# A decoder trunk on one core: compression's first unit, its cache copies, the third sequence's pages and gelu's table

## The reference

```python
h = x @ w_in                                  # q, k, v of all heads, gate logits
o_A = dilated window attention (8 heads)
# compression: 32 rows of 64, every 16 rows, of the paged cache and of the new rows
blk = rows[:, idx] + pe[:, None, :]
kc  = gelu(blk @ w1) @ w2                     # likewise vc
o_B = gated sum of compressed, selected (top 16 blocks) and window attention
x = LayerNorm(alpha*x + concat(o_A, o_B) @ w_o)
x = LayerNorm(alpha*x + PEER(x))              # top 16 of 128*128 experts per head
```

## Time and profile before

| what | us |
|---|---|
| median of 3 runs (1332.22 to 1334.04) | 1333.13 |
| the profiled execution's own time | 1332.8 |
| its span in the trace | 1331.0 |
| TensorE busy in the span | 1271.3 (96%) |
| VectorE | 974.2 (73%) |
| ScalarE | 573.7 (43%) |
| GpSimd | 294.5 (22%) |
| mean granted TensorE clock | 0.987 of full |

### The profile page before, as it was taken

One profiled execution on the slowest core, in us unless ns is written; L12 is line 12 of the kernel. 1 busy time (PEld: TensorE's weight loads), 2 busy tenths in 40 slices (PEclk: granted clock), 3 DMA queues, 4 the chain that ended last, 5 costly groups with the idle time before them and its releaser, 6 DMA issues.

```text
span 1331.0 us, 25923 instructions
## 1 busy us (share of the span) xinstructions
PE 1271.3 (96%) x8435; PEld 1081.4 (81%) x8436; DVE 974.2 (73%) x2220; ACT 573.7 (43%) x1058; POOL 294.5 (22%) x521
## 2 busy tenths in 40 slices
PE   9998599989899999999999999999999999999996
PEld 6888588866554777889998889889889888988985
DVE  4664366546634399989988887887888788888886
ACT  4643366534421211124345454454455444444453
POOL 0004132040001288711121111111122112212101
PEclk9998799999999999999999999999999999999998
DMA  8756577788974487859939999989988999998962
GB/s 289 225 160 190 167 248 243 261 276 325 403 303 167 144 285 287 290 199 260 287 122 330 318 311 315 319 312 312 321 309 308 323 312 309 322 317 301 324 196 92
DMA packets 164384, 358.79 MB, mean 270 GB/s; under 512 B 49235, under 2 KB 99091, under 8 KB 160595
## 3 DMA queue, kind: packets, MB, share of 16 engines
q1 hardware_dynamic: 134562, 242.51, 53.8%
q0 software_dynamic: 25424, 111.37, 23.9%
q10 hardware_dynamic: 4320, 3.93, 0.9%
HBM read 341.56 MB, written 53.35 MB: 297 GB/s over the span
## 4 chain that ended last, share of the span: by engine, by line
PE 50%; DVE 4%; issue 2%; DVEq 1%; ACT 1%; POOLq 0%; POOL 0%; ACTq 0%
PE psum L1918 25%; PE psum L1907 7%; PE psum L1906 7%; PE psum L1905 7%; PE psum L1427 2%; PE psum L1931 2%; DVE gated_i L2066 2%; DVE v_lo L2079 0%; DVEq L2066 0%; ACT v_hi L1987 0%; DVE OT L2062 0%; DVE ln_bn L1354 0%; DVE x L1348 0%; DVE gated_lo L2115 0%; DVE x L1377 0%
## 5 line engine op out<-in xcount | busy, mean ns | idle before, releaser
L1907 PE MATMUL psum<-x_hi,u_lo 128*128 128x256 f32 x760 | 215.1, 283 | 0.0
L1906 PE MATMUL psum<-x_lo,u_hi 128*128 128x256 f32 x760 | 215.0, 283 | 0.0
L1905 PE MATMUL psum<-x_hi,u_hi 128*128 128x256 f32 x760 | 214.6, 282 | 0.0
L2079 DVE TENSOR_TENSOR v_lo<-big,v_hi 128x1024 fp32r<-128x1024 f32 x128 | 156.7, 1224 | 35.1 <-ACT v_hi L1987 33.8
L1987 ACT ACTIVATE v_hi<-big 128x1024 fp32r<-128x1024 f32 x128 | 135.3, 1057 | 83.1 <-PE psum L1918 80.9
L1918 PE MATMUL psum<-v_hi,gated_hi 128*128 128x512 f32 x512 | 159.9, 393 | 1.1 <-DVE gated_lo L2115 1.0
L1918 PE MATMUL psum<-v_lo,gated_hi 128*128 128x512 f32 x512 | 158.7, 390 | 0.0
L1918 PE MATMUL psum<-v_hi,gated_lo 128*128 128x512 f32 x512 | 158.3, 390 | 0.0
L1906 PEld LDWEIGHTS psum<-x_lo,u_hi 128*128 128x128 f32 x760 | 145.5, 191 | 3.7
L1905 PEld LDWEIGHTS psum<-x_hi,u_hi 128*128 128x128 f32 x760 | 145.5, 191 | 3.7
L1907 PEld LDWEIGHTS psum<-x_hi,u_lo 128*128 128x128 f32 x760 | 145.5, 191 | 0.0
(11 more groups left out here) (323 smaller groups left out, 2518.8 us busy)
## 6 DMA issues: line engine op xcount, KB each, us to landing
big<-in_peer_v SPq DMA_DIRECT2D x128, 512.0 KB
big<-in_peer_u SPq DMA_DIRECT2D x115, 512.0 KB, 5.1
w_then_a_vals<-in_a_v SPq DMA_DIRECT2D x8, 2048.0 KB
keep_ak<-in_a_k POOLq DMA_DIRECT2D x32, 508.0 KB, 6.3
keep_av<-in_a_v POOLq DMA_DIRECT2D x24, 512.0 KB, 7.4
big<-in_a_k SPq DMA_DIRECT2D x4, 2048.0 KB, 13.3
a_keys<-in_a_k SPq DMA_DIRECT2D x4, 2048.0 KB, 12.4
wq_ring<-in_peer_wq SPq DMA_DIRECT2D x16, 512.0 KB, 5.6
```

What stands on the lines that cost most here:

```text
L1905: pe.matmul(H[:, 0:SEQ], uh[:, q, kc], x1h[:, k, :], start=(k == 0), stop=False)
L1906: pe.matmul(H[:, 0:SEQ], uh[:, q, kc], x1l[:, k, :], start=False, stop=False)
L1907: mm = pe.matmul(H[:, 0:SEQ], ul[:, q, kc], x1h[:, k, :], start=False, stop=(k == KD - 1))
L2079: ve.tensor_tensor(vl[:, q], vs[:, q], vh[:, q].bitcast(F32), ALU.subtract).then_inc(s["v_lo"], 1)
```

## The change

Four edits, all in the functions above:

- VectorE makes U0's quarters 1, 2 and 3 one after the other at the start of compression. Its gates come behind the bias copies.
- GpSimd's copies: none in U0 and U5; 32 (numbers 48 to 79) in U1 to U4, two per step, and ahead of steps 1 to 3 a wait for TensorE's step before. Numbers 32 to 47 go to the first norm, four ahead of each right part and four behind the last.
- The selected pages of sequence 2 are issued by ScalarE, two in each of four steps from U6's step 2 to U7's step 1, behind a wait for the prompt's last scores.
- ScalarE runs gelu on one column of a small tile of its own ahead of the real gelu in step 3, so that the table is loaded without the waits for TensorE and for the bias. The tile is filled once with a copy.

```diff
-def load_sel_pages(eng, t, d, s, b):
-
-    for p in range(PAGES):
+def load_sel_pages(eng, t, d, s, b, places=range(PAGES)):
+
+    for p in places:
         r = eng.value_load(t.ptab[0:1, b * PAGES + p:b * PAGES + p + 1], min_val=0, max_val=79)
...
+        warm = sb("gelu_warm", [P, 2])
...
             sp.dma_start(t.ka[1], d.a_k[1]).then_inc(s["ld_ka1"], 16)
-            load_sel_pages(sp, t, d, s, 2)
             sp.wait_ge(s["pages_lo"], 4 * NUC)
             load_sel_pages(sp, t, d, s, 1)
...
                 for j in range(4):
-                    for x in range(2 if u < 6 else 0):
-                        keep_copy(gp, d, s, 32 + 8 * u + 2 * j + x)
+                    if 1 <= u < 5:
+                        if j:
+                            rows_used(gp, u, j - 1)
+                        for x in range(2):
+                            keep_copy(gp, d, s, 48 + 8 * (u - 1) + 2 * j + x)
...
+            act.activation(warm[:], t.c0[:, 0:2], ACT.Copy).then_inc(s["warm"], 1)
+            act.wait_ge(s["warm"], 1)
...
                     if j == 3:
+                        act.activation(warm[:, 1:2], warm[:, 0:1], ACT.Gelu_apprx_tanh)
                         for h in range(2):
                             gelu(u, h)
...
                     prompt(u, j)
+                    if 4 * u + j >= CHOICE and 4 * u + j < CHOICE + 4:
+                        if 4 * u + j == CHOICE:
+                            act.wait_ge(s["p_scores"], NU)
+                        load_sel_pages(act, t, d, s, 2, range(2 * (4 * u + j - CHOICE), 2 * (4 * u + j - CHOICE) + 2))
...
                         if j == 0:
-                            split_pages_lo(ve, t, s, 0, 1)
+                            for y in range(1, 4):
+                                split_pages_lo(ve, t, s, 0, y)
                         turned_out(4 * j)
                         turned_out(4 * j + 2)
                         if j == 0:
                             evac_last(ve, t, s, len(WCOLS) - 1)
-                        if j < 2:
-                            split_pages_lo(ve, t, s, 0, 2 + j)
                         if j == 2:
                             own_lo(ve, t, s, 1)
-                        if j == 3:
-                            gates()
...
+                    if (u, j) == (0, 3):
+                        gates()
...
             for i in range(TILES):
+                for x in range(4):
+                    keep_copy(gp, d, s, 32 + 4 * i + x)
                 norm.right(gp, i)
+            for x in range(12, 16):
+                keep_copy(gp, d, s, 32 + x)
```

More of the change, by code:

```diff
@@ L2273 @@
         "keep_wk": (NB, P, 512 - NT), "keep_wv": (NB, P - 2, 4 * P)}
-FRONT_SEMS = """x_in0 x_in1 x_in2 x_in3 w_hi w_lo w_used h_low proj w_in0 w_in1 w_in2 c0 w1k w1v w1_hi w1_lo w2 idle own_hi own_lo pages_hi pages_lo rows_used cmp_first evac roped out0 out_kv gate gate_e gate_a
+FRONT_SEMS = """x_in0 x_in1 x_in2 x_in3 w_hi w_lo w_used h_low proj w_in0 w_in1 w_in2 c0 w1k w1v w1_hi w1_lo w2 idle warm own_hi own_lo pages_hi pages_lo rows_used cmp_first evac roped out0 out_kv gate gate_e gate_a
 turned turned_out turned_act rope_c cmp_pg0 cmp_pg1 cmp_bias cmp_turn cmp_hid cmp_gelu cmp_second cmp_done""".split()
```

## The result

| | before | after |
|---|---|---|
| median of 4 runs each, us | 1332.78 (1332.22 to 1334.04) | 1314.07 (1312.16 to 1314.47) |
| the profiled execution's own time | 1332.8 | 1312.16 |
| its span | 1331.0 | 1310.3 |
| mean granted clock | 0.987 | 0.995 |

The ratio of after to before is 0.9858, with a 95% interval of 0.9846 to 0.987: 18.7 us faster, for a forecast of 1315.0. (Before's median is over four runs here, 1332.78; the 1333.13 in front of the prediction was over three of them.) The profiled execution of after is the fastest of its four, so the two traces lie 20.7 us apart, 2 more than the medians.

A forecast was written before the change was run, and what follows sets the result against it. Bound: TensorE's stops in compression and the slow clock behind them, the largest from copies delaying U2's pages. -2.5 - 17.95 - 2.3 + 4.6 = -18.1 us from 1332.8 gives 1314.7, 1315.0 as median; range 1308 to 1323.

The forecast's parts named there:

- U1 begins: Compression: with gelu's table loaded early and the gates later, unit U1 begins at 115.15, a gain of 2.5 us.
- U1 lasts: Compression: unit U1 runs as one piece, 18.7 us in place of 36.65, so 17.95 us go.
- U2 to U7, clock: Compression: U2's first 24 products no longer run at the lower clock level, so 2.3 us go.
- ScalarE's pages, stop: Ahead of U7: a pair of page issues before U6's gelu makes U7 begin 2.3 us later.
- ScalarE's pages, clock: Behind the stop ahead of U7: half clock follows and adds 2.3 us.
- norm's copies: First norm: 16 copies, 24 us of DMA, fit into 24 free us; nothing taken, up to 1 us either way.
- The gelu part: Ahead of U1: ScalarE loads the table from 113.0 and starts the real gelu at about 114.5; gain 2.5 us.
- A: Ahead of U7: ScalarE's issues are cheap or the clock holds, 0.7 in place of 4.6 us, 1311; chance 0.2.
- B: Compression: the page chain becomes the bound, up to 9.5 us back, about 1323; chance 0.13.
- C: First norm: moved copies hold it up, GpSimd's issues waiting for VectorE, 11 us, time 1326; chance 0.03.
- D: Behind the norm: the copies' 24 us of DMA push later loads one for one, 1339, slower; chance 0.03.
- The slowest landing: Compressed pages' loads in the new profile: maximum landing under 8 us, median 2 to 3 us.

The follow-up runs named there:

- copies_only: Kernel before plus only the copies' new places (none in U0 and U5, 32 in U1 to U4, 16 in the first norm): 1313.98 us, ratio 0.9869.
- old_copies: Changed kernel with the copies as before (48 in U0 to U5, unpaced, none in the norm): 1324.80 us, ratio 0.9954 to before.
- no_warm: Changed kernel without the little gelu ahead of the real one: 1317.64 us, ratio 0.9896 to before.
- sp_pages: Changed kernel with sequence 2's pages issued by SP as before: 1310.32 us, ratio 0.9830 to before.
- late_pages: Changed kernel with ScalarE's page issues one step later, the first pair behind U6's gelu: 1312.20 us, ratio 0.9855 to before.
- old_split: Changed kernel with U0's low parts made one per step as before: 1320.21 us, ratio 0.9907 to before.
- after_again: The changed kernel, unaltered, timed once more in the third session: 1314.55 us, ratio 0.9870 to before.
- pages_only: Kernel before with only sequence 2's pages moved to ScalarE: 1335.09 us, ratio 1.0026.
- unpaced: Changed kernel without GpSimd's waits for TensorE's steps, same number and places of copies: 1314.60 us, ratio 0.9872 to before.
- split_only: Kernel before with only U0's low parts made at once: 1321.11 us, ratio 0.9919.
- exp_late_sp: Changed kernel with sequence 2's pages on SP and ScalarE's block-score exponential moved behind U6's gelu: 1308.21 us, ratio 0.9831 to before.

## Why the prediction was right

**The bound and the cause.** TensorE's stops in compression, with the slow clock behind them, were what there was to win here, and the burst of copies made U2's pages late: shown by copies_only and old_copies.

**Step by step**, at the milestones of the traces:

| term | predicted | measured |
|---|---|---|
| U1 begins | 115.15 (-2.5) | 115.14 |
| U1 lasts | 18.7 (-17.95) | 19.39, of it 0.74 the stop ahead of U2 (-17.26) |
| U2 to U7, clock | -2.3 | -2.56 (107.55 to the stop ahead of U7, before 110.11) |
| ScalarE's pages, stop | +2.3 | +2.02 |
| ScalarE's pages, clock | +2.3 | +1.17 (U7 to attention 19.24, before 18.07) |
| sum at sample attention | -18.1 | -19.14 |
| norm's copies | 0 | 0 |

U2 does not begin at 133.8 but at 134.53, with 0.74 us of stop in front. I had the bias at about 132.3 with the table already loaded; in the trace the bias is there at 133.12, and the load ahead of U2 starts only at 132.49, behind an exponential and a split of ScalarE, so that gelu begins at 133.90.

The gelu part is right to 0.1 us on each engine: load at 113.10 (113.0), gelu at 114.50 (114.5). The load took 1.28 us, and the little gelu follows 1.29 us after its start. "ScalarE: Activation LUTs", What ACT_TABLE_LOAD costs, in the Trainium skill, adds a drain of 1380 ns; neither this row nor no_warm, where the switch moved U1 by 1.15 us and not by 2.7, shows one.

**What was mis-sized: the price of ScalarE's pages.** I took 4.6 us, and from before to after it is 3.2 at the milestones, or 3.5 if the slow products are counted. A pair of issues holds ScalarE for 1.82 us (the idle time ahead of 243.64), not 2.2. And the slow stretch behind the stop is 16 products, from 247.07 on, not 24: the first 6 still go at full clock. (250.46 - 247.07) - 16 x 0.12 = 1.5 us, not 2.3. With 3.5 in place of 4.6 the sum gives 1313.9. That the clock's part is the pages' doing is not shown: taking the pages off ScalarE (sp_pages, late_pages) brought back 2.1 us at sample attention, about the stop alone, and behind the 2.27 us that were left the clock fell as well.

**How much is luck.** The forecast's pieces were off by up to 1.4 us and in both directions (U1 lasted 0.7 us longer, the pages cost 1.1 to 1.4 us less), and sample attention varies by up to 2.7 us over the traces. The forecast lies 0.9 us from the median, which is less than that, so the closeness of the total is in part luck; the table is the better test. Two small slips of the working change nothing: 14 x 0.5 + 2 x 0.25 is 7.5, not 7.6 MB, and U2's last page left at 121.83, not 121.4.

**Rivals.** A (cheap issues) needed a stop of 2 us ahead of U7; it is 4.21, and sp_pages shows the 2 us between. B (the page chain as bound) did not happen: between 135 and 242 TensorE stands for less than 0.2 us. But old_split shows how near it is, and in after_again ScalarE waits 1.34 us for U3's last page (at 142.87), which TensorE does not feel. I costed the early splits as a matter of timing; they are what keeps the chain of U2 free, and I had put no price on their absence. C and D are refuted: no right part of the norm waits for GpSimd's issues. The share in the window rises by (0.93 - 0.45) x 44 = 21 us of DMA, TensorE is busy for the same 42.29, and all that follows the routing's first product is as long as before. The 24 free us held. The trap of "SBUF — State Buffer" in the Trainium skill does not show here either: the two pairs took 1.10 and 0.99 us. But VectorE ran the norm's sums and moments beside them (from 395.64 on) and no plain copy, so these rows are a weak test of it.

**Signs that missed.** The slowest landing is 10.9 us, not under 8. No copy of GpSimd is near it: it is U7's first page, right behind SP's own two loads of 2 MB. ScalarE waits for no page in this trace. I had looked for collisions with GpSimd's copies only and had left these loads out.

## What to carry to other kernels

Background copies without a deadline can delay the small loads of a running stage to several times their usual landing time (20.5 us against a median of 3.0 here); put them where the share of DMA is low and the next load has slack, and check by an experiment that takes the copies away alone. On the engine whose output the bound engine waits for, the order of the program is what counts: a pair of DMA issues or an exponential that waits belongs behind that output, not ahead of it (2 us of TensorE's stop for the pair and 2.27 for the exponential, in the traces). And parts of a change depend on each other: making one stage start earlier can make another part necessary, so take parts out of the finished kernel as well as adding them one by one.

## What I had not expected of the hardware

- The clock can fall behind stops of some 2 us, and often not at once. After stops of 2.27 us (sp_pages, late_pages), 2.38 (no_warm), 3.52 (pages_only) and 4.21 us (after), between 2 and 11 products ran at full clock first, and then 12 to 16 at half. In unpaced, behind the same 4.21 us, the half clock is there from the first product, and ahead of U1 in before it came inside the stop (granted clock 1.00 until 115.85, 0.50 from there).
- The length of the last stop does not decide it. After 2.19 us (before, copies_only, split_only) the clock did not fall, and neither after 2.89 us in old_copies (1.00 from 128 to 137). But in exp_late_sp it did within 1.1 us of a stop of 1.98 us. So I can't say that the 0.08 us between 2.19 and 2.27 made the difference in sp_pages.
- How long it stays down varies between executions. Behind the same stop of 3.71 us the half clock lasted for 12 products in split_only (117.67 to 120.47) and for 22 in copies_only (to 122.87). That alone moves single traces against each other by 1 us, and I had taken 24 products as the rule from the one row of U2 in before.
- Three of the four pairs of page issues on ScalarE show as 1.8 us of idle time ahead of the next instruction. The second is issued while the table load and gelu run (244.56 and 245.69) and does not show.
- A part can cost more than its length: the table's load of 1.3 us came to 3.2, because the clock fell behind the longer stop and because it stood in the way twice, ahead of U1 and of U2.
